# A two-block transformer kernel on one core: fewer zero products, vector loads behind the second weight chunk, the first chunk in quarters, and a value piece projected with the weights stationary

## The reference

```python
def first_block(x, attn_pre_g, w_in, swa_sinks, ...):
    h = rms_norm(x, attn_pre_g[layer])
    proj = jnp.einsum("bsd,de->bse", h, w_in[layer])          # 1024 x 2304
    q_a, k_a, v_a, q_b, k_b, v_b = jnp.split(proj, IN_SPLITS, axis=-1)
    # widths:  512,  128,  128,  512,  512,  512
    y_a = swa_sink_attention(q_a, k_a, v_a, swa_sinks[layer], swa_slopes)   # window 128, 8 heads, 2 of k, v
    y_a = rms_norm(y_a, swa_out_g[layer])
    lam = exp(sum(diff_lq1 * diff_lk1)) - exp(sum(diff_lq2 * diff_lk2)) + lambda_init
    y_b = diff_attention(q_b, k_b, v_b, lam, diff_slopes, diff_subln_g[layer], lambda_init)
    mix = jnp.concatenate([y_a, y_b], axis=-1)
    x = x + rms_norm(mix @ w_out[layer], attn_post_g[layer])
    x = x + rms_norm(conv_ffn(rms_norm(x, ffn_pre_g[layer]), w_up, conv_w, conv_b, w_down), ffn_post_g[layer])
    return x
# second_block(x, c_2, ...): modulation, dilated and stick-breaking attention, 32 experts (top 2), final norm
```

## Time and profile before

| | |
|---|---|
| median of 3 runs | 1006.81 us (1004.8 to 1008.15) |
| the profiled execution | 1006.47 us |
| its span, first to last instruction | 1004.8 us, so 1.67 lie around it |
| TensorE busy | 983.8 us, 98% |
| VectorE, ScalarE, GpSimd busy | 54%, 34%, 8% |
| chain that ended last | TensorE 88%, DMA 5%, VectorE 3%, ScalarE 1% |
| granted TensorE clock, mean | 0.997 |

### The profile page before, as it was taken

The page is one execution under the profiler, slowest core; times in us unless marked ns, Lnnn a source line. Parts: engine busy times, 40 slices in busy tenths (PEclk is TensorE's granted clock), DMA queues, the critical chain, the costliest instruction groups (busy, mean ns, idle before and its releaser), DMA issues.

```text
span 1004.8 us, 15368 instructions
## 1 busy us (share of the span) xinstructions
PE 983.8 (98%) x5945; PEld 684.9 (68%) x5945; DVE 547.2 (54%) x1051; ACT 346.5 (34%) x579; POOL 79.3 (8%) x119
## 2 busy tenths in 40 slices
PE   8999999999999998999999999999999999999997
PEld 6998799999999996889865544444444444444433
DVE  6478789889999997848425322222221222222222
ACT  5665675444554563556332111111110111111102
POOL 8200101011111200200001000000000000000000
PEclk9999999999999999999999999999999999999999
DMA  8424467788788754444938899999999999999994
GB/s 305 169 84 168 162 223 263 282 307 321 296 304 332 271 187 154 162 168 168 379 123 272 339 402 420 424 430 427 428 427 429 427 426 429 429 429 430 428 424 183
DMA packets 60024, 312.17 MB, mean 311 GB/s; under 512 B 4125, under 2 KB 5514, under 8 KB 47434
## 3 DMA queue, kind: packets, MB, share of 16 engines
q1 hardware_dynamic: 52160, 284.83, 70.8%
q0 software_dynamic: 7392, 26.54, 7.5%
q10 hardware_dynamic: 426, 0.16, 0.1%
HBM read 310.47 MB, written 1.05 MB: 310 GB/s over the span
## 4 chain that ended last, share of the span: by engine, by line
PE 88%; DMA 5%; DVE 3%; ACT 1%; issue 1%; POOL 0%; SPq 0%; DVEq 0%; ACTq 0%
PE bank L925 13%; PE bank L927 12%; PE bank L926 12%; PE bank L1498 10%; PE bank L1479 10%; PE bank L1531 10%; PE bank L1406 6%; DMA eslots<-in_w_gate 4%; PE bank L1072 3%; PE bank L1415 3%; DMA ring<-in_w_in 2%; PE bank L1000 1%; PE bank L1038 1%; DVE ring_r L1984 1%; PE bank L1509 1%
## 5 line engine op out<-in xcount | busy, mean ns | idle before, releaser
L925 PE MATMUL bank<-hT_r,ring_r 128*128 128x256 f32 x664 | 189.4, 285 | 1.5 <-DVE ring_r L1984 1.5
L927 PE MATMUL bank<-hT_r,ring_r 128*128 128x256 f32 x664 | 187.9, 283 | 0.0
L1984 DVE TENSOR_TENSOR ring_r<-ring,ring_r 128x2048 fp32r<-128x2048 f32 (+1 forms) x74 | 164.7, 2260 | 14.3 <-ACT ring_r L1613 13.9
L1613 ACT ACTIVATE ring_r<-ring 128x2048 fp32r<-128x2048 f32 (+1 forms) x74 | 136.5, 1888 | 39.6 <-DMA ring<-in_w_up 34.4
L926 PE MATMUL bank<-v_tok_r,ring_r 128*128 128x256 f32 x496 | 140.4, 283 | 0.0
L925 PEld LDWEIGHTS bank<-hT_r,ring_r 128*128 128x128 f32 x664 | 127.4, 192 | 2.3 <-DVE ring_r L1984 1.7
L927 PEld LDWEIGHTS bank<-hT_r,ring_r 128*128 128x128 f32 x664 | 127.3, 192 | 0.0
L1531 PE MATMUL bank<-eslots,scratch 128*64 128x512 f32 x496 | 113.4, 595 | 0.7 <-ACT scratch L1864 0.7
L926 PEld LDWEIGHTS bank<-v_tok_r,ring_r 128*128 128x128 f32 x496 | 95.2, 192 | 0.2
L927 PE MATMUL bank<-ring_r,hn_r 128*128 128x512 f32 (+2 forms) x236 | 87.1, 369 | 0.0
L1531 PEld LDWEIGHTS bank<-eslots,scratch 128*64 128x64 f32 x496 | 35.7, 137 | 62.8 <-issue 61.6
(11 more groups left out here) (337 smaller groups left out, 1522.4 us busy)
## 6 DMA issues: line engine op xcount, KB each, us to landing
eslots<-in_w_gate SPq DMA_DIRECT2D x31, 2048.0 KB, 21.4
eslots<-in_w_up SPq DMA_DIRECT2D x30, 2048.0 KB, 19.3
eslots<-in_w_down SPq DMA_DIRECT2D x28, 2048.0 KB, 23.4
ring<-in_w_up SPq DMA_DIRECT2D x16, 2048.0 KB, 11.8
ring<-in_w_in SPq DMA_DIRECT2D x9, 2048.0 KB, 8.1
ring<-in_w_down SPq DMA_DIRECT2D x8, 2048.0 KB, 9.0
kT<-in_w_ada POOLq DMA_DIRECT2D x24, 512.0 KB, 7.5
ring<-in_w_out SPq DMA_DIRECT2D x4, 2048.0 KB, 8.3
```

Source lines behind the costliest of these rows:

```text
L925: pe.matmul(dst, lhs[0], rhs[0], start=start, stop=False, **flags)
L927: return pe.matmul(dst, lhs[1], rhs[0], start=False, stop=stop, **flags)
L1613: sc.activation(hi, raw, ACT.Copy).then_inc(s_whi, 1)
L1984: last = ve.tensor_tensor(lo, raw, hi, ALU.subtract)
```

## The change

The names of lines in the order rows below are those of each kernel's own file.

1. TensorE: the six zero products go, the three become one.
2. Chunk 0 comes in two quarters and a half in place of two halves. ScalarE and VectorE split each quarter as it comes, and project_first starts with the first.
3. The twelve vector loads go from ScalarE's queue to SP's, behind chunk 1 and ahead of chunk 2.
4. ka is made by `project_rounded_first`: the 16 products of the rounded weights, which wait for ScalarE alone, then the eight of `lo`.
5. Item 5 (vT) makes v with the weights stationary and all 256 tokens moving: 24 products of 256 columns, not 48 of 128. VectorE copies the result, which is v transposed, to PT, and a new item 7 (turn) is two transpositions by TensorE behind the first scores, taken by VectorE into v_tok. The items behind it have a number that is one higher, so ScalarE and VectorE swap them (VectorE now takes turn, q1, q2, k2, v0; ScalarE k0, k1, q3, k3, v1).
6. Two semaphores are merged (s_c into s_vec), and the waits on counts follow.

```diff
-        items1 += [(1, "ka", (0, 0)), (1, "v", (P, P, 0))]
+        items1 += [(1, "ka", (0, 0)), (1, "vT", (P, 0))]
...
-        items1 += [q_item(0), k_item(0), q_item(1), k_item(1), q_item(2), q_item(3), k_item(2), k_item(3), v_item(0),
+        items1 += [q_item(0), (1, "turn", (0, 0)), k_item(0), q_item(1), k_item(1), q_item(2), q_item(3), k_item(2), k_item(3), v_item(0),
                    v_item(1)]
...
-        BETWEEN = [{0: [7], 1: [8], 2: [9], 3: [10], 4: [11], 5: [12], 6: [13], 7: [14], 8: [15]},
+        V_TURNED = 7
+        BETWEEN = [{0: [7, 8], 1: [9], 2: [10], 3: [11], 4: [12], 5: [13], 6: [14], 7: [15], 8: [16]},
...
+            if kind == "vT":
+                return [(PT[:, 0, 0:S], bank[:, 0:S])]
+            if kind == "turn":
+                return [(vt[:, :, 0:P], bank[:, 0:S].rearrange("p (t n) -> p t n", t=T))]
...
-            for half, done in enumerate((s_loaded_once, loaded[0])):
-                tiles_of_half = slice(half * KD // 2, (half + 1) * KD // 2)
-                sp.dma_start(raw[:, tiles_of_half, :], w_in[:, tiles_of_half, 0:HALF]).then_inc(done, 16)
-            for c in range(1, LANES):
-                straight(N_IN + c, w_in[:, :, c * HALF:(c + 1) * HALF])
+            for first, end, done in ((0, 2, s_loaded_once), (2, 4, loaded[SLOT_N + 3]), (4, KD, loaded[0])):
+                sp.dma_start(raw[:, first:end, :], w_in[:, first:end, 0:HALF]).then_inc(done, 16)
+            straight(N_IN + 1, w_in[:, :, HALF:2 * HALF])
...
+            sp.dma_start(stage[:, 0, :], cw[0:P, :]).then_inc(s_stage, 16)
+            sp.dma_start(stage[0:FT, 1, :], cw[P:P + FT, :]).then_inc(s_stage, 16)
+            sp.dma_start(stage[FT:2 * FT, 1, :], cb).then_inc(s_stage, 16)
+            for name, row in (("c_2", R_C), ("attn_pre_g", R_PRE), ("ffn_pre_g", R_FPRE), ("g_mix_2", R_MIX),
+                              ("g_ffn_2", R_FFN), ("swa_out_g", R_SWA), ("g_dil_out_2", R_DIL),
+                              ("g_sb_out_2", R_SB), ("diff_subln_g", R_SUB)):
+                v = a[name].rearrange("o (f p) -> (o f) p", p=P)
+                sp.dma_start(stage[row:row + v.shape[0], 2, :], v).then_inc(s_stage, 16)
+            straight(N_IN + 2, w_in[:, :, 2 * HALF:3 * HALF])
...
+                if kind == "turn":
+                    piece_taken(blk, AHEAD[0])
+                    for t in range(T):
+                        last = pe.transpose(bank[:, t * P:(t + 1) * P], PT[:, 0, t * P:(t + 1) * P], ident[:, :])
+                    last.then_inc(s_gemm[blk], 1)
+                    return
...
+                        if blk == 0 and n == 0:
+                            piece_taken(blk, V_TURNED + 1)
...
-            stay_awake(PS[7], 6)
             turn("attn1", hn, range(T - 1))
 
-            stay_awake(PS[6], 3)
+            stay_awake(PS[6], 1)
...
+            def project_rounded_first(n):
+
+                c, kind, (c0, _) = items1[n]
+                assert kind == "ka" and n < AHEAD[0]
+                w = split_view((N_IN + c) % LANES)
+                dst = item_bank(0, n)[:, 0:S]
+                pe.wait_ge(s_whi, 2 * (N_IN + c) + 2)
+                for k in range(KD):
+                    for part in range(2):
+                        pe.matmul(dst, w[0][:, k, c0:c0 + P], tiles("attn1", k)[part],
+                                  start=(k == 0 and part == 0), stop=False)
+                split_ready(N_IN + c)
+                for k in range(KD):
+                    last = pe.matmul(dst, w[1][:, k, c0:c0 + P], tiles("attn1", k)[0], start=False,
+                                     stop=(k == KD - 1))
+                last.then_inc(s_gemm[0], 1)
...
-            split_one(N_IN, 0)
+            for quarter, (done, ready) in enumerate(((s_loaded_once, s_whi_first), (loaded[SLOT_N + 3], s_whi))):
+                sc.wait_ge(done, 16)
+                raw, hi, _ = first_quarter(quarter)
+                sc.activation(hi, raw, ACT.Copy).then_inc(ready, 1)
```

More of the change, by code:

```diff
@@ L287, in two_block_kernel @@
         s_lame = sem("s_lame")
-        s_c = sem("s_c")
+        s_whi_first = sem("s_whi_first")
         s_ms = sem("s_ms")
@@ L438, in split_part, with first_quarter @@
             return view(ring, lane), view(ring_r, LANES + lane), view(ring_r, lane)
+        def first_quarter(quarter):
+            return [view[:, quarter * SLOT_W // 4:(quarter + 1) * SLOT_W // 4]
+                    for view in (ring[:, 0, :], ring_r[:, LANES, :], ring_r[:, 0, :])]
         QB0 = SWA_Q * HD + 2 * SWA_KV * HD
@@ L568, in needs @@
                 return AHEAD[0]
-            return (15 if values else 10) if i < 9 else (16 if values else 14)
+            return (16 if values else 11) if i < 9 else (17 if values else 15)
         def turned(u):
@@ L955, in project @@
                     flags = dict(start=(k == 0), stop=(k == KD - 1))
-                    if kind in ("q", "k", "ka"):
+                    if kind in ("q", "k", "ka", "vT"):
                         c0 = where[1] if kind == "q" else where[0]
@@ L1161, in project_first @@
                 first, second = range(KD // 2), range(KD // 2, KD)
-                pe.wait_ge(s_whi, 1)
-                rounded_products(first, 0)
-                pe.wait_ge(s_wlo_first, 1)
-                rounded_products(first, 1)
+                quarters = (range(2), range(2, 4))
+                for ks, rounded_part in zip(quarters, (s_whi_first, s_whi)):
+                    pe.wait_ge(rounded_part, 1)
+                    rounded_products(ks, 0)
+                for n, ks in enumerate(quarters):
+                    pe.wait_ge(s_wlo_first, n + 1)
+                    rounded_products(ks, 1)
                 low_products(first)
@@ L1179, in _ @@
             turn_gains()
-            for n in range(4, AHEAD[0] + 1):
+            project_rounded_first(4)
+            for n in range(5, AHEAD[0] + 1):
                 if n == AHEAD[0]:
@@ L1567, in then @@
                 sc.wait_ge(s_alink, order[0])
-            cw = a["conv_w"].rearrange("o j (f p) -> (o j f) p", p=P)
-            cb = a["conv_b"].rearrange("o (f p) -> (o f) p", p=P)
             sc.dma_start(pre_rows, a["attn_pre_g"].rearrange("o (f p) -> (o f) p", p=P)).then_inc(s_pre, 16)
-            sc.dma_start(stage[:, 0, :], cw[0:P, :]).then_inc(s_stage, 16)
-            sc.dma_start(stage[0:FT, 1, :], cw[P:P + FT, :]).then_inc(s_stage, 16)
-            sc.dma_start(stage[FT:2 * FT, 1, :], cb).then_inc(s_stage, 16)
-            for name, row in (("c_2", R_C), ("attn_pre_g", R_PRE), ("ffn_pre_g", R_FPRE), ("g_mix_2", R_MIX),
-                              ("g_ffn_2", R_FFN), ("swa_out_g", R_SWA), ("g_dil_out_2", R_DIL),
-                              ("g_sb_out_2", R_SB), ("diff_subln_g", R_SUB)):
-                v = a[name].rearrange("o (f p) -> (o f) p", p=P)
-                sc.dma_start(stage[row:row + v.shape[0], 2, :], v).then_inc(s_stage, 16)
             def scaled(tag, scale, shift=None):
@@ L1607, in split_one @@
             def split_one(n, part, more=0):
-                if n == N_IN and part == 0:
-                    sc.wait_ge(s_loaded_once, 16)
-                elif n == N_IN or part == 0:
+                if n == N_IN or part == 0:
                     sc.wait_ge(loaded[n % LANES], 16 * (n // LANES + 1) + 16 * more)
@@ L1738, in _ @@
             split(seq_gate(0) + 1)
-            sc.activation(siluc, vec[:, 2, R_C:R_C + KD], ACT.Silu).then_inc(s_c, 1)
+            sc.activation(siluc, vec[:, 2, R_C:R_C + KD], ACT.Silu).then_inc(s_vec, 1)
             def taps(i, part, b):
@@ L1986, in split_one @@
                     last.then_inc(s_wlo, 1)
-                elif n == N_IN:
-                    last.then_inc(s_wlo_first, 1)
             def take(blk, pieces):
@@ L2221, in _ @@
             ve.wait_ge(s_vec, 1)
-            split_one(N_IN, 0)
+            for quarter, rounded_part in enumerate((s_whi_first, s_whi)):
+                ve.wait_ge(rounded_part, 1)
+                raw, hi, lo = first_quarter(quarter)
+                ve.tensor_tensor(lo, raw, hi, ALU.subtract).then_inc(s_wlo_first, 1)
             low("attn1", lambda k: pre_gain[:, k:k + 1])
@@ L2317, in _ @@
             ve.wait_ge(s_ada0, 16)
-            ve.wait_ge(s_c, 1)
+            ve.wait_ge(s_vec, 3)
             ve.nop().then_inc(s_sum, 8)
```

4 lines of the change are left out of this document (3 added, 1 removed).

## The result

| | before | after |
|---|---|---|
| median, 20 runs each | 1006.31 us | 1007.76 us |
| ratio to before | | 1.0017 (95%: 1.001 to 1.0024) |
| the profiled execution | 1006.47 us | 1006.68 us |
| start of k0 on TensorE | 37.75 us | 35.26 us |
| first product of w_out (`out_projection`) | 90.06 us | 90.56 us |

The change was forecast to give 3 us. It gained 2.5 us up to k0, nearly as forecast, and lost all of it and 0.5 more between 70 and 91 us, a stretch in which the prediction had read VectorE's waits as slack and nothing else.

What follows compares the result with a forecast made beforehand. TensorE was taken to hold the chain from a little after 18.1 us to 86.38, so a gain at k0 would stay. 1006.47 − 3.05 (k0 from 37.75 to 34.7, chunk 2's landing 0) = 1003.4 us, range 1001.9 to 1006.4.

Steps and rivals of the forecast that it cites:

- what sets k0: VectorE's copy and second `lo`, behind chunk 2's split on ScalarE, let k0 start at 34.7, not 37.75: 3.05 us.
- the waits in front of q0 and the scores: TensorE idles some 0.4 before q0 for ScalarE's takes and 0.4 before the scores for VectorE's copy.
- The value piece: On TensorE before q0: 24 products of 256 columns replace 48 of 128, 2.4 us less than 5.31.
- the first product: TensorE's first real product starts at about 10.5 instead of 12.24, 1.7 us earlier.
- chunk 2's landing: Arrival of chunk 2 at ScalarE, 23.84 before: taken as unchanged (0), bounds up to 1.3 earlier and +5.4.
- the slower rival: Twelve small loads at 0.5 each delay chunk 2 by 5.4; k0 at 40.1, time 1008.8; chance 0.09.
- the starved queue: SP issues the twelve loads slowly, so chunk 2 is issued at 18.7, after chunk 1's data ended: 1005.9; chance 0.12.
- What is gained there stays: After k0, later waits on other engines and weight-load releases move with TensorE's scores, so the gain at k0 is kept.
- turn's own copy: VectorE's second 128x256 copy, due before the first PV: costs nothing beside VectorE's 8.7 us of waits, otherwise 0.43.
- it doesn't show: Something later (second block's loads, experts' weights) keeps its own time and takes the gain back: 1006.5; chance 0.05.
- The last of the signs of being wrong: k0 at 34.7 with the time still above 1005 would mean a later wait and a wrong prediction.
- The clock rival: Fewer zero products drop TensorE to 1.2 GHz at the start, adding 2.4 us there; k0 at 36.0, 1004.7; chance 0.13.

Runs made afterwards that it cites:

- wait_added: Kernel before plus one VectorE wait: in attention step 7 it waits for v0 before splitting w_out's first chunk; 1009.35 us, ratio 1.0039.
- again: The changed kernel rerun unaltered as a control, against the kernel before; 1006.13 us, ratio 1.0011.
- vt_only: Kernel before with only the transposed value piece and its turn, nothing else of the change; 1006.77 us, ratio 1.0007 to the kernel before.
- split_first: Changed kernel with VectorE, in attention step 7, splitting w_out's first chunk before taking v0; 1004.45 us, ratio 0.9991 to the kernel before.
- start_only: Changed kernel without the transposed value piece and turn, numbering as in the kernel before; 1004.57 us, ratio 0.9989 to the kernel before.
- late_again: Repeat of the changed kernel with VectorE's w_out split first and ScalarE's and VectorE's chain behind chunk 2 loosened; 1002.66 us, ratio 0.9973 to before.

## Why the prediction was wrong

**Right:** what sets k0, and nearly its size. k0 was forecast at 34.7 and came at 35.26. The chain behind chunk 2 took 10.85 us against the 10.86 of the sum (34.7 − 23.84), and the waits in front of q0 and the scores were there. The value piece was 2.9 us. Each part on TensorE held within 0.6 us: the first product was forecast at 10.5 and came at 11.08, because the second quarter reached ScalarE at 9.52, took 1.06 rather than 0.95, and the first hT_r piece took another 0.6. Nothing hung on it.

**A term that was mis-sized:** chunk 2's landing. I took 0; it was 24.41 against 23.84 in this profile, with the dip of the flow at 16 to 19 us. Over all profiles ScalarE had it between 23.72 and 24.09 with the old loads (six, mean 23.9), and between 23.90 and 24.82 with the new ones (eight, mean 24.3). The small loads cost some 0.4 us, not the 5.4 of the slower rival. The row of 8 to 9 us, from which the 0 was argued, had them on another queue than the large ones. The slower rival and the starved queue fell.

**The step that failed** is one sentence: "What is gained there stays: the later waits on other engines hang on TensorE's scores and move with them". It was argued from waits in the trace of before, where VectorE waits for TensorE, and that view was read up to 86 us only as slack. But the change does not only shift the work; the new item changes who takes every item behind it. In its place the runs showed a new wait of VectorE for TensorE's v0 (4.85 us) ahead of its own split, and 55.3 us from k0 to w_out in place of 52.3.

The prediction costed turn's own copy (0.43) and no other step that changed hands. The description of the change had the fact ("VectorE now takes turn, q1, q2, k2, v0"), and the order of VectorE shows v0's take directly in front of the two halves of w_out's split. It could have been costed from the trace of before. There v0's products end at about 78.2. (wait_added, whose TensorE is 0.15 ahead, has VectorE begin the split at 78.06.) The take and the split, 0.6 and 4.4 us, would put the logits at about 83.2, and they came at 79.10. That is 4.1 us late, more than the whole gain. How much of it would reach TensorE could not be read off; the runs say 3.0. The rival that came nearest, "it doesn't show", had 0.05 and looked for the cause in the loads. The last of the signs of being wrong, a k0 near 34.7 with a time still above 1005, is the one that came true.

**Why it was slower, and not the same.** The profiles show 0.5 us lost at 90 us; the ratio says 1.7 (1.0 to 2.4). `again`, the same kernel, gave 1.1 (−0.2 to 2.5), and vt_only, with 0.2 lost at that point, 0.7. The remaining 0.5 us or more was not located, and its cause stays open. Chunk 2's landing is a candidate, since it moves k0 and differs between executions; one profile each does not show it. Part of the scatter between single executions is known, and it bars a closer reading of one profile each: see the last section.

**The clock rival** was half seen. In split_first TensorE had idled 1.74 us and ran its transpositions at half the pace:

```profile
8.45 1.78 PE L922 MATMUL bank<-ident,hn 128*128 128x128 f32 x8 [1.74 <-DVE hn L2257]
10.03 0.63 PE L904 MATMUL bank<-zrow 128*128 128x512 bf16 x1
10.45 1.85 PE L922 MATMUL bank<-ident,hn 128*128 128x128 f32 x8
```

and the windows of TensorE alone (stretch, busy, granted clock, DMA share, GB/s) show 1.2 GHz there and 2.4 GHz again for the products:

```profile
8.50:9.50 1.00, 1.00 (x6) 0.60 1.04 395
10.50:11.50 1.00, 1.00 (x6) 0.50 1.03 397
12.00:13.00 1.00, 1.00 (x10) 0.94 1.05 393
```

It cost the start some 0.9 us (first product at 12.02, against 11.16 in `again`) and k0 nothing, as the chain behind chunk 2 was later still. The clock came back after nothing but sixteen transpositions and one zero product, and in the row of 547 to 551 us it had stayed up over little else than transpositions. The Trainium skill, "TensorE: Matmul & The Clock Gate", "Part 4: PE-mode transpose", says that transpositions do not count as busy in the same way. These rows do not agree with it. With the twelve small loads ahead of it chunk 2 came 0.1 to 1.0 us later than in the profile of before. The Trainium skill, "DMA: Bandwidth & Descriptors", "Bandwidth", gives 0.95 us for one load of 64 KB, issued by GpSimd, which for twelve is an estimated 11 us. The trace does not agree with that either.

## What to carry to other kernels

Where engines share work by the parity of a counter, an item put in changes hands of everything behind it; for each step that moves to another engine, look at what is queued behind it there and when its input comes. Slack that an engine shows in waits can be used up at once if the wait comes to stand in front of its own work instead of behind it: do independent work first, then take. And do not count on a gain at one point of the chain being kept where the change also alters the order, or the owner, of work on another engine further on: read that engine's order up to the next wait on it.

## What the runs showed of the hardware

TensorE idles 2.56 us once in all of these kernels, with an end between 383 and 392 us. What follows differs from one execution to the next. These are windows of TensorE alone (stretch, busy, granted clock, DMA share, GB/s) in the kernel before, after, and `again`, the latter two being the same code:

```profile
388.00:389.00 1.00, 1.00 (x4) 0.50 1.03 403
```
```profile
388.00:389.00 1.00, 1.00 (x5) 0.91 1.07 416
389.00:390.00 1.00, 1.00 (x4) 0.50 1.03 403
```
```profile
388.00:389.00 1.00, 0.89 (x4) 1.00 1.04 395
389.00:390.00 1.00, 1.00 (x6) 1.00 1.05 410
```

After the same pause the clock fell to 1.2 GHz for some 3 us in the first two, directly or a little later, and stayed at 2.4 GHz in the third. Of all fourteen profiles it fell there in eight. Three us at half the pace are 1.5 us, as much as the whole effect under study, so no single profile's total can be set against another's here; starts of the same instruction at one early point can. Chunk 0's first quarter, 0.5 MB behind 1 MB of x, reached ScalarE between 7.34 and 8.65 us, a spread of 1.3 us for the same loads in the same order (start_only and late_again).
